# The delta rule's decay sums as rows in DRAM, broadcast to 128 partitions by one transfer per head pair and tile

## The reference, cut to what matters

```python
g = -jnp.exp(a_log) * jax.nn.softplus(a + dt_bias)      # (B, T, H), per direction
g_cum = jnp.cumsum(g, axis=2)                           # within a chunk
diff = g_h[..., :, None] - g_h[..., None, :]            # g_cum[t] - g_cum[s]
decay = jnp.where(incl, jnp.exp(jnp.where(incl, diff, 0.0)), 0.0)
l_strict = jnp.where(strict, einsum('bnthd,bnshd->bnhts', k_beta, k) * decay, 0.0)
t_inv = triangular_solve(eye + l_strict, eye)           # per chunk and head
att = jnp.where(incl, einsum('bnthd,bnshd->bnhts', q, k) * decay, 0.0)
```

## Time and profile before

| | us |
|---|---|
| median of 3 runs | 2361.31 (2359.95 to 2364.9) |
| the profiled execution | 2353.64 |
| its span on the core | 2351.6 |
| PE busy / weight loads | 2167.6 / 1468.8 |
| DVE, ACT, POOL busy | 931.7, 846.4, 358.0 |

### The profile page before, as it was taken

The page is one execution under the profiler, slowest core; times in us unless marked ns, Lnnn a source line. Parts: engine busy times, 40 slices in busy tenths (PEclk is TensorE's granted clock), DMA queues, the critical chain, the costliest instruction groups (busy, mean ns, idle before and its releaser), DMA issues. The chain is left out here.

```text
span 2351.6 us, 31435 instructions
## 1 busy us (share of the span) xinstructions
PE 2167.6 (92%) x10970; PEld 1468.8 (62%) x10970; DVE 931.7 (40%) x2271; ACT 846.4 (36%) x2205; POOL 358.0 (15%) x591
## 2 busy tenths in 40 slices
PE   6999899899979989999999999988988968899998
PEld 3676576555545776555674437766575657766787
DVE  2023364656563325333331120246667653243321
ACT  2223253535443224444231112245346443244421
POOL 1000007071542000000000010000742760000000
PEclk8999899999989999999999999999999989999999
DMA  8215312211212022111222342122321312223243
GB/s 290 68 58 171 101 39 66 80 51 47 81 28 64 28 63 82 55 46 37 73 73 89 107 149 77 34 73 67 95 64 55 89 38 73 63 92 110 90 143 126
DMA packets 191419, 190.14 MB, mean 81 GB/s; under 512 B 28559, under 2 KB 185955, under 8 KB 190755
## 3 DMA queue, kind: packets, MB, share of 16 engines
q1 hardware_dynamic: 186048, 171.08, 23.5%
q0 software_dynamic: 3648, 16.72, 2.2%
q10 hardware_dynamic: 1571, 0.34, 0.1%
HBM read 178.62 MB, written 9.50 MB: 80 GB/s over the span
## 5 line engine op out<-in xcount | busy, mean ns | idle before, releaser
L1042 PE MATMUL bank<-hT,ring 128*128 128x512 f32 (+2 forms) x1856 | 727.1, 542 | 5.5 <-DMA ring<-in_w_in_dram 3.5
L1042 PEld LDWEIGHTS bank<-hT,ring 128*128 128x128 f32 (+1 forms) x1856 | 335.4, 192 | 256.1 <-issue 237.7
L1042 PE MATMUL bank<-ring,hT 128*128 128x256 f32 (+2 forms) x2112 | 458.5, 373 | 25.0 <-DMA ring<-in_w_in_dram 25.0
L1042 PE MATMUL bank<-WORK 128*128 128x128 f32 (+4 forms) x3056 | 403.7, 289 | 73.8 <-ACT WORK L1672 21.0
L1042 PEld LDWEIGHTS bank<-WORK 128*128 128x128 f32 (+3 forms) x3056 | 324.9, 172 | 188.9 <-issue 139.4
L1042 PEld LDWEIGHTS bank<-ring,hT 128*128 128x128 f32 x2112 | 385.8, 193 | 88.1 <-issue 35.6
L1042 PE MATMUL bank<-yT,ring 128*128 128x512 f32 (+1 forms) x768 | 273.4, 490 | 0.0
L1042 PEld LDWEIGHTS bank<-yT,ring 128*128 128x128 f32 x768 | 139.5, 193 | 80.2 <-issue 71.1
L1007 POOL TENSOR_TENSOR WORK<-WORK 64x31 f32<-64x31 f32 (+15 forms) x248 | 149.5, 603 | 19.4
L1977 DVE SCALAR_TENSOR_TENSOR WORK<-WORK,CW 128x512 f32<-128x512 f32 (+1 forms) x192 | 146.7, 764 | 3.0
L1005 POOL TENSOR_TENSOR WORK<-WORK 64x31 f32<-64x31 f32 (+15 forms) x248 | 139.5, 562 | 19.5
(11 more groups left out here) (202 smaller groups left out, 2071.0 us busy)
## 6 DMA issues: line engine op xcount, KB each, us to landing
ring<-in_w_in_dram SPq DMA_DIRECT2D x92, 1024.0 KB, 5.4
ring<-in_ada_w_dram SPq DMA_DIRECT2D x24, 1024.0 KB, 6.4
ring<-in_w_branch_dram SPq DMA_DIRECT2D x24, 1024.0 KB, 5.2
ring<-in_w_out_dram SPq DMA_DIRECT2D x8, 1024.0 KB, 5.0
ring<-in_mla_q_up_dram SPq DMA_DIRECT2D x8, 576.0 KB, 4.0
xs<-yT POOLq DMA_DIRECT2D x2, 2048.0 KB, 10.6
ring<-in_mla_kv_up_dram SPq DMA_DIRECT2D x8, 512.0 KB, 4.7
yT<-xs POOLq DMA_DIRECT2D x2, 2048.0 KB, 10.0
```

Source lines behind the costliest of these rows:

```text
L1042: return nc.tensor.matmul(o, a, b, start=start, stop=stop, skip_group_check=True)
```

## The change

The cumulative sums are no longer made per pair and tile by PE. Once a layer a new item `dgr`, four plan places after `dg`, turns `GC` by four transposes on PE, ACT copies the 16 rows to `GT`, and SP writes them to DRAM (`GD`, eight transfers of 4 KB). For each `d1` SP then issues one transfer that reads a pair's four rows of 128 (2 KB) once for every partition and writes the 256 KB straight into the slot of `DC`. DVE's four instructions take their input from `DC` where they took it from PSUM. `d1` has no part on PE and holds no bank.

```diff
-    return it[0] in ("ab", "abT", "dg") or it[0] in ("dqkv", "cv", "dsilu", "dsil2", "dnq", "dn") and it[2] == 0
+    return it[0] in ("ab", "abT", "dg", "dgr") or it[0] in ("dqkv", "cv", "dsilu", "dsil2", "dnq", "dn") and it[2] == 0
...
-        return [("ab", l)] + out[:4] + [("abT", l)] + out[4:10] + [("dg", l)] + out[10:]
+        return [("ab", l)] + out[:4] + [("abT", l)] + out[4:10] + [("dg", l)] + out[10:14] + [("dgr", l)] + out[14:]
...
-         "dd": 0, "dt": 0, "sol": 0, "dv": 0, "dw": 0, "dg": 2}
+         "dd": 0, "dt": 0, "sol": 0, "dv": 0, "dw": 0, "dg": 2, "d1": 0}
...
+        GD = nc.dram_tensor("GD", (DEPTH, 4, TT, 4, P), F32, kind="Internal").ap()
+        GT = SLA[96:112, 0:512].rearrange("p (t n) -> p t n", t=TT)
...
+        def decay_held(it):
+            mine = [i for i in kinds["d1"] if i[1] == it[1] and i[3] % 2 == it[3] % 2]
+            n = mine.index(it)
+            return mine[n - 1] if n else None
...
-            todo += [(where[it], 1, 0, it) for it in plan if it[0] in ("dg", "dt")]
+            todo += [(where[it], 1, 0, it) for it in plan if it[0] in ("dg", "dgr", "dt")]
+            todo += [(where[("dd",) + decay_held(it)[1:]] if decay_held(it) else where["dgr", it[1]], 2, 0, it)
+                     for it in kinds["d1"]]
...
+                elif u[0] == "dgr":
+                    sp.wait_ge(*done(u, "act"))
+                    for g in range(4):
+                        for r in range(2):
+                            sp.dma_start(GD[l, g, :, 2 * r:2 * r + 2].rearrange("t u n -> u t n"),
+                                         GT[r * BH + 2 * g:r * BH + 2 * g + 2, :, :]).then_inc(s_rows, 16)
+                elif u[0] == "d1":
+                    _, l, g, tt = u
+                    held = decay_held(u)
+                    if held:
+                        sp.wait_ge(*done(("d2",) + held[1:], "dve"))
+                        sp.wait_ge(*done(("dd",) + held[1:], "act"))
+                    else:
+                        sp.wait_ge(*done(("norm", l), "pe"))
+                        sp.wait_ge(s_rows, 128 * (l + 1))
+                    sp.dma_start(DC[:, tt % 2, :],
+                                 GD[l, g, tt].rearrange("u n -> (u n)").partition_broadcast(P)).then_inc(s_dc[tt % 2], 16)
@@ in the program of PE @@
+                elif k == "dgr":
+                    pe.wait_ge(*done(("dg", l), "dve"))
+                    for tt in range(TT):
+                        ins = tr(ps[0:16, tt * P:(tt + 1) * P], GC[:, tt, :])
...
-                elif k == "d1":
-                    _, l, g, tt = it
-                    pe.wait_ge(*done(("dg", l), "dve"))
-                    for r in range(2):
-                        for hh in range(2):
-                            u = 2 * r + hh
-                            ins = mm(ps[:, u * P:(u + 1) * P],
-                                     col(GG, tt, g, u).broadcast_to([P, P]), kc(C_TRI + r * P))
@@ in the program of ACT @@
+                elif k == "dgr":
+                    ins = nc.scalar.activation(GT, ps[0:16, :].rearrange("p (t n) -> p t n", t=TT), ACT.Copy)
@@ in the program of DVE @@
                 elif k == "d1":
                     dve.wait_ge(*done(("dg", l), "dve"))
+                    dve.wait_ge(s_dc[tt % 2], 16 * decay_round(it))
                     for u in range(4):
                         c = slice(u * P, (u + 1) * P)
-                        ins = V_.scalar_tensor_tensor(DC[:, tt % 2, c], ps[:, c], col(GC, tt, g, u), kc(C_NEG + (u // 2) * P),
-                                                      ALU.subtract, ALU.min)
+                        ins = V_.scalar_tensor_tensor(DC[:, tt % 2, c], DC[:, tt % 2, c], col(GC, tt, g, u),
+                                                      kc(C_NEG + (u // 2) * P), ALU.subtract, ALU.min)
```

More of the change, by code:

```diff
@@ L370 @@
            "gb": ("act",), "gatt": ("dve",), "gw": ("dve",), "go": ("act", "dve"),
-           "ab": ("dve",), "abT": ("dve",), "dg": ("act", "dve"), "dqkv": ("act",), "dn": ("act",), "d1": ("dve",),
+           "ab": ("dve",), "abT": ("dve",), "dg": ("act", "dve"), "dgr": ("act",), "dqkv": ("act",), "dn": ("act",),
            "d2": ("dve",), "d3": ("act", "dve"), "dx": ("dve",), "dya": ("dve",), "dyb": ("act",), "dx6": ("dve",),
@@ L663, in hybrid_block @@
         s_beta = stack.enter_context(nc.semaphore("beta_rows_out"))
+        s_rows = stack.enter_context(nc.semaphore("decay_rows_out"))
+        s_dc = [stack.enter_context(nc.semaphore(f"decay_rows_in{i}")) for i in range(2)]
         s_lout = stack.enter_context(nc.semaphore("l_out"))
@@ L711, in hybrid_block @@
                  "dt", "sol", "dv", "dx", "dya", "dx6", "sk", "sq", "su", "sa"}
-        NODVE = {"norm", "osq", "dqkv", "pc", "dnq", "xin", "gqk", "gv", "lr", "mp", "xout", "mkT",
+        NODVE = {"dgr", "norm", "osq", "dqkv", "pc", "dnq", "xin", "gqk", "gv", "lr", "mp", "xout", "mkT",
                  "dd", "sol", "dw", "dyb", "st"}
@@ L717, in hybrid_block @@
                 continue
-            if k not in ("nx", "nh", "cv", "dsilu", "dsil2", "dnq", "osq", "z2", "rstd", "dd", "dt", "sol", "dv", "dw"):
+            if k not in ("nx", "nh", "cv", "dsilu", "dsil2", "dnq", "osq", "z2", "rstd", "d1", "dd", "dt", "sol", "dv", "dw"):
                 parts["pe"].add(k)
@@ L841, in scan_left, with decay_round @@
                     eng.wait_ge(*done(i, who))
+        def decay_held(it):
+            mine = [i for i in kinds["d1"] if i[1] == it[1] and i[3] % 2 == it[3] % 2]
+            n = mine.index(it)
+            return mine[n - 1] if n else None
+        def decay_round(it):
+            return [i for i in kinds["d1"] if i[3] % 2 == it[3] % 2].index(it) + 1
         def systems(dram):
@@ L940, in _ @@
                                          BT[r * BH + 2 * g:r * BH + 2 * g + 2, :, :]).then_inc(s_beta, 16)
+                elif u[0] == "dgr":
+                    l = u[1]
+                    sp.wait_ge(*done(u, "act"))
[14 more added lines that the diff above has]
+                                 GD[l, g, tt].rearrange("u n -> (u n)").partition_broadcast(P)).then_inc(s_dc[tt % 2], 16)
                 else:
```

## The result

| | before | changed |
|---|---|---|
| median | 2358.51 us (2350.04 to 2364.9, 8 runs) | 2368.36 us (2365.43 to 2373.51, 8 runs) |
| the profiled execution / its span | 2353.64 / 2351.6 | 2366.41 / 2364.6 |
| mean granted TensorE clock in it | 0.969 | 0.958 |

The ratio is 1.0045, 95% interval 1.0028 to 1.0062: the change costs 10.6 us, with 6.6 to 14.6 as bounds. The forecast was 2368, on a before of 2361.3, so +6.8.

What follows compares the result with a forecast made beforehand. PE, 92% busy, was taken to bound the kernel only where no wait for another chain follows. First layer 0.0 and second +6.8, on a median of 2361.3, gave 2368; 8 in 10 range 2347 to 2390.

Steps and rivals of the forecast that it cites:

- The three kinds of place: First layer's first head, where PE runs through; inversions with a head, awaiting DVE's copy; heads that something later must await.
- The products removed: 32 groups of PE products, 33.6 us: -4.2 for the first layer's first head's four, nothing for the other 28.
- The term at nothing: The 28 groups outside the first layer's first head: without them PE only arrives earlier and waits longer, 0 us.
- PE's time comes back: Rival: all 33.6 us of products less 1.2 come off, 2329; chance 0.06 for all, 0.15 for part.
- middle case: Only the first layer's heads count, -16.8 for products, about -12 in sum: 2349; chance of PE's time partly back 0.15.
- The landing: DVE waits at tiles 2 and 3 for a 256 KB transfer, 3.5 us: +2.3, four times +0.9, two times +1.8.
- The second and third rival: Short landing of 2.5 us, no change, 2361 to 2363, chance 0.22; slow landing of twice 3.5, 2392, chance 0.14.
- the estimate of 2.6: Skill's formula for landing 256 KB, 2.0 us plus bytes over 436 GB/s; by it the sum would be near +0.5.
- The signs that failed: In the changed profile: PE about 34 us less busy, idle up by more, its wait for DVE's copy some 3 longer.
- The term that was too small: DVE's waits for landing, 2.3, four 0.9s and two 1.8s; PE's restarts, 1.9 us a time, counted only in the range.
- the forecast's own case: Landing between 1.7 and 4.3 us, PE restarts at the lower clock included: 2358 to 2380.

Runs made afterwards that it cites:

- first_only: The kernel before, changed in the first layer's first head alone; the other 28 product groups stay on PE and are read: 2353.9 us, 0.9978 of before.
- no_dma: The changed kernel without the 32 broadcast transfers and DVE's waits for them, decays made from old slot contents: 2353.3 us, 0.9981 of before.
- keep28: `slots4` with PE's products kept, unread, in all heads but the first layer's first (28 groups): 2351.7 us, 0.9972 of before.
- slots4: The changed kernel with four decay slots instead of two, so transfers go one head ahead and DVE waits for no landing: 2354.4 us, 0.9984 of before.
- twice28: `keep28` with the four products of each of its 28 groups done twice, unread, 29.4 us more PE work: 2354.9 us, 0.9985 of before.
- late: The changed kernel with the next head's transfers behind this head's last `LD` writes in SP's queue: 2368.4 us, 1.0049 of before.
- slots4_late: `slots4` with the next head's transfers behind this head's last `LD` writes: 2353.7 us, 0.9989 of before.
- pe_kept2: The changed kernel with all 32 groups of PE's products kept, DVE waiting for them, results unread: 2370.9 us, 1.0058 of before.
- slots4b: `slots4` run again, on the same chip as `keep28b`: 2353.3 us, 0.9981 of before.
- double: The changed kernel, but at tiles 2 and 3 an equal extra transfer must land before the real one is issued: 2406.7 us, 1.0209 of before.
- keep28b: `keep28` run again, on the same chip as `slots4b`: 2351.2 us, 0.9970 of before.

## Why the prediction came out

**What bounds the kernel: right.** PE is 92% busy, and yet 29.4 us of its time can be put in for about 4 us. The three kinds of place were the right cut.

**The products removed: right in the main.** The sum had -4.2 for the four of the first layer's first head and nothing for the 28. `first_only` and `no_dma` show the first (-5.2 and -4.5 with the 0.6 in it), `keep28` against `slots4` and `twice28` that the 28 bring nothing. The term at nothing left something out: without the 28 the kernel is 2.7 us slower (with 2.4 to either side), not equal, and its clock is lower. *PE's time comes back*, the first rival, falls with its middle case.

**The landing: right in kind, near in size.** 3.5 assumed, 3.3 measured. Before's profile had a nearer row than those used, GpSimd's load of `LD`, also 256 KB, with 3.3; and one of 2.9, its write of `XD`. Idle times of DVE: 0.97, 0.41, 0.76, 0.95 where I had 0.9 four times; 1.83 and 2.17 in the fourth heads (two rows each) where I had 1.8; 1.91 in the second layer's first head for 2.3. Sum 9.0 against 9.5. In the stretches from a layer's first `d1` to its last `dv` the changed kernel and `late` stand 12.3 us above before in the mean of both, the three profiles with four slots 2.0: 10.3 for the waits and what follows from them. The second and third rival, a landing under 2.5 and one of 7, are both out, and the estimate of 2.6 with them.

**The signs that failed.** PE was to be about 34 us less busy and its idle time up by more than that. It is 11.4 less busy and 24.4 more idle. PE's wait for DVE's copy was to be some 3 us longer in each of the four inversions with a head in them. It is 4.07, 2.16, 1.66 and 1.92, where before had 2.80, 1.99, 2.80 and 2.80. Part of it stands at the group of 64x64 before that one, and the two waits together grew by 5.7 over the four. Both signs took the time of PE's remaining work as fixed, and the same records took longer.

**The term that was too small.** By the ratios the wait costs 14 us, not 9.5: 0.0061 between changed and `slots4`, 0.0060 between `late` and `slots4_late`, and 0.0086 between `pe_kept2` and `keep28`, which less the 4.2 of the first head is 16. Each has some 4 us to either side; that three pairs say the same makes the missing 5 us or so likely. I had put what PE loses on restart in the range and not in the sum. The terms as measured, -5.2 for the first head, +2.7 for the other 28 and +14 for the wait, make 11.5 where the change cost 10.6.

The clocks of all executions bear on it: 0.955 to 0.960 in the 14 of the changed kernel and `late`, 0.957 to 0.966 in the 33 with four slots, whose means are 0.958 and 0.962. So the wait lowers the mean clock too. The rows to look at are those of the four inversions with a head in them. The same 32 and 20 records of PE behind its wait for DVE's copy in the first layer's second head, in the changed kernel:

```profile
466.98 1.51 PE L1076 MATMUL bank<-WORK 64*64 64x64 f32 x32 [4.07 <-DVE WORK L2091]
468.42 10.12 PE L1076 MATMUL bank<-hT,ring 128*128 128x512 f32 x20
```

With four slots, in `slots4` and then in `slots4b`:

```profile
468.90 1.17 PE L1082 MATMUL bank<-WORK 64*64 64x64 f32 x32 [2.98 <-DVE WORK L2097]
470.00 8.85 PE L1082 MATMUL bank<-hT,ring 128*128 128x512 f32 x20
```

```profile
465.57 2.00 PE L1082 MATMUL bank<-WORK 64*64 64x64 f32 x32 [2.98 <-DVE WORK L2097]
467.50 10.97 PE L1082 MATMUL bank<-hT,ring 128*128 128x512 f32 x20
```

Before it was 1.17 and 8.85, and 10.55 in the third head. The same work takes 8.85 or up to 2.1 more, and the same kernel shows either. The granted clock was 1.00 from 468.9 to 478.8 in `slots4` and 0.76 from 465.6 to 478.4 in `slots4b`. Summed over the four inversions and the four groups of 64x64, x8, 64x64 and x20 in each, what lies above the shortest of each is, with the wait, 11.2 us in the changed kernel, 12.2 in `late`, 8.5 in `double` and 7.3 in `pe_kept2`. Without it, it is 5.9, 4.7 and 5.8 with four slots; 3.1 in `no_dma`; 1.7, 5.1, 1.8 and 5.0 in `keep28`, `keep28b`, `twice28` and `first_only`; 1.7 before. In the four kernels with the wait all four inversions have such a place, in the others one to three. The 6 us between 11.7 and 5.5 are of the size of what is missing. That they are the missing part is argued and not shown, and the cause of the missing 5 us stays open. No kernel here changes the clock alone. `pe_kept2` stands only 3.9 above the mean of `keep28` and `keep28b`, where 7 are missing. `double`, with the longest waits and the lowest clock, has less of it than the changed kernel, and its added waits cost no more than themselves. And one profile stands for most kernels, where two profiles of one kernel differ by 7 us of span (`slots4` 2355.5 and 2348.5, `keep28` 2349.0 and 2356.1).

**Why 2368 was met more closely than its terms.** The forecast added 6.8 to a median of three runs, 2361.3. Before's median over its later runs is 2358 to 2358.5, so the change cost 10, and the time came out at 2368 because a baseline too high by 3 and a cost too low by 4 made it up. That is luck. The range of the forecast's own case, 2358 to 2380, held both.

**The version to take.** `first_only` and `keep28` both beat before, by 5 and 7 us. `first_only` is the plain one of the two, since it makes no product that nobody reads: the rows serve one head of eight, the only one in which PE runs through.

## What to carry to other kernels

Ahead of taking work off a 92% busy engine, find for each place the wait that comes next on it: where that wait is for a chain which doesn't pass through the engine, the work is worth nothing, and doubling it is a cheap test of that. On PE look at the clock as well: here it fell when idle time took the place of work. A transfer in place of products is free as long as its slot comes free one stage ahead; two slots short, it costs its landing less the time in which the reader was busy anyway, once for each use, and here some 5 us more that the sum of these waits doesn't explain. Take the sum's baseline from as many runs as the result's, and never one profile each for a difference of 3 us. The granted clock of every execution tells more than that of the one profiled.

## What the hardware showed that I had not expected

A transfer that reads one 2 KB row of DRAM for each of 128 partitions landed in 3.3 us, no slower than the 256 KB with 128 rows of their own (3.5): reading one place over and over cost nothing here. Only in `slots4_late`, where a head's four go out in a row, did they take longer (medians): 3.9 into `SQ` and 5.4, for the later two, into `MT`. The `LD` writes behind such transfers in SP's queue landed later: 2.2 us in the changed kernel and `keep28`, 2.1 in `slots4`, 1.9 in `late`, and 1.7 as before in `no_dma`, `first_only` and `slots4_late`, where none goes out ahead of them or, in `first_only`, only in one head of eight. DVE's subtraction took as long from SBUF as from a PSUM bank, where the estimate in the prediction had 65 ns less. In before's profile the 128 instructions had a mean of 341 ns; their group in the changed kernel:

```profile
L2040 DVE SCALAR_TENSOR_TENSOR SQ<-SQ,WORK,K 128x128 f32<-128x128 f32 x128 | 35.9, 345 | 12.0 <-DMA SQ<-GD 10.9 <-issue 0.9
```
